# Recurrent preparation: another order of the bonus factor, the rows of r and k, the exponentials and the key norm's root

## What is computed

```
w = -softplus(-(w0 + tanh(xw @ w_lora1) @ w_lora2)) - 0.5;  log_decay = -exp(w)
a = sigmoid(a0 + (xa @ a_lora1) @ a_lora2)
kk = heads(k * k_k)
kk = kk / maximum(sqrt(sum(kk * kk, axis=-1)), 1e-12)      # the key norm
k = k * (1 + (a - 1) * k_a)
y = scan(r, log_decay, k, v, -kk, kk * a)                  # state of 64 x 64 per head
bonus = sum(r * k * r_k, axis=-1) * v
```

## Time and profile before

| | us |
|---|---|
| median of 3 runs (lowest to highest) | 4425.35 (4421.27 to 4426.27) |
| profiled execution | 4427.14 |
| its span, first to last instruction | 4425.4 |
| PE busy in the span | 4140.4 (94%) |
| VectorE busy | 3212.2 (73%) |
| ScalarE busy | 1564.6 (35%) |
| GpSimd busy | 698.8 (16%) |

### The profile page before, as it was taken

One profiled execution on the slowest core, in us unless ns is written; L12 is line 12 of the kernel. 1 busy time (PEld: TensorE's weight loads), 2 busy tenths in 40 slices (PEclk: granted clock), 3 DMA queues, 4 the chain that ended last, 5 costly groups with the idle time before them and its releaser, 6 DMA issues. The chain is left out here.

```text
span 4425.4 us, 62371 instructions
## 1 busy us (share of the span) xinstructions
PE 4140.4 (94%) x23580; PEld 3705.0 (84%) x23580; DVE 3212.2 (73%) x4912; ACT 1564.6 (35%) x2731; POOL 698.8 (16%) x580
## 2 busy tenths in 40 slices
PE   8999989978988999898978999999999999999995
PEld 6888875657766877787767999999999999999995
DVE  4444437757835445699095889988999999889997
ACT  2111213436623322222373333333333333333333
POOL 0000001113310100234500111111111111111110
PEclk9999999999999999899999999999999999999998
DMA  9999996886786487674368999999999999999996
GB/s 277 316 313 315 313 268 176 246 244 184 209 216 212 129 253 223 206 220 143 128 173 273 313 322 321 312 317 317 314 315 321 319 317 317 315 315 318 318 316 215
DMA packets 609083, 1176.94 MB, mean 266 GB/s; under 512 B 113944, under 2 KB 363648, under 8 KB 554160
## 3 DMA queue, kind: packets, MB, share of 16 engines
q1 hardware_dynamic: 534992, 800.28, 61.6%
q0 software_dynamic: 54256, 363.92, 21.7%
q10 hardware_dynamic: 19568, 9.18, 0.8%
HBM read 1006.90 MB, written 228.15 MB: 279 GB/s over the span
## 5 line engine op out<-in xcount | busy, mean ns | idle before, releaser
L102 PE MATMUL h_ps<-h_a,h_v 128*128 128x352 f32 x6144 | 1080.7, 324 | 22.5 <-DVE h_a L96 12.6
L102 PE MATMUL h_ps<-xs,h_ut 128*128 128x352 f32 x6144 | 1078.2, 324 | 17.3 <-DVE h_ut L96 17.3
L102 PEld LDWEIGHTS h_ps<-h_a,h_v 128*128 128x128 f32 x6144 | 1005.4, 189 | 31.5 <-DVE h_a L96 17.8
L102 PEld LDWEIGHTS h_ps<-xs,h_ut 128*128 128x128 f32 x6144 | 1010.7, 188 | 18.0 <-DVE h_ut L96 18.0
L102 PE MATMUL a_ps<-xt_hi,a_w 128*128 128x512 f32 x1792 | 553.1, 390 | 8.0 <-DVE a_w L96 8.0
L96 DVE TENSOR_TENSOR h_v<-h_v_raw,h_v 128x512 fp32r<-128x512 f32 x512 | 350.3, 684 | 73.7 <-ACT h_v L95 73.6
L102 PEld LDWEIGHTS a_ps<-xt_hi,a_w 128*128 128x128 f32 x1792 | 337.1, 188 | 78.3 <-issue 8.2
L95 ACT ACTIVATE h_v<-h_v_raw 128x512 fp32r<-128x512 f32 x512 | 318.2, 622 | 215.5 <-PE h_ps L102 212.4
L102 PE MATMUL a_ps<-xt_lo,a_w 128*128 128x512 f32 x896 | 349.2, 390 | 0.0
L2810 DVE SCALAR_TENSOR_TENSOR y_first<-h_rows,h_acts,y_first 128x2048 f32<-128x2048 f32 x128 | 300.2, 2345 | 0.0
L2804 DVE CUSTOM_DVE_ANT_0 h_rows<-h_rows,h_x_first 128x2048 f32<-128x2048 f32 x128 | 292.2, 2283 | 0.0
(11 more groups left out here) (385 smaller groups left out, 6452.7 us busy)
## 6 DMA issues: line engine op xcount, KB each, us to landing
h_v_raw<-in_peer_v SPq DMA_DIRECT2D x128, 1024.0 KB, 10.0
h_u_raw<-turned_d SPq DMA_DIRECT2D x138, 512.0 KB, 10.2
raw_d<-in_peer_u SPq DMA_DIRECT2D x472, 128.0 KB, 3.8
h_u_raw<-raw_d SPq DMA_DIRECT2D x118, 512.0 KB, 9.9
a_raw<-in_w_in SPq DMA_DIRECT2D x28, 2048.0 KB, 12.8
a_xin<-in_peer_u SPq DMA_DIRECT2D x224, 256.0 KB, 8.1
turned_d<-a_xin SPq DMA_DIRECT2D x56, 1024.0 KB, 7.0
yt_last<-sums_d SPq DMA_DIRECT2D x124, 176.0 KB, 5.3
```

Of the source, the lines that this page charges most:

```text
L102: mm = pe.matmul(out, lhs[a], rhs[b], start=(first and n == 0), stop=(last and n == 2))
```

## The change

The order inside a turn changes on two engines; no instruction is added or taken away. On ScalarE the three exponentials stand ahead of the root. On VectorE `rk_part` stands right behind `k_new`, ahead of the lower halves of "square"; `r_row`, `k_row` and `decay_end` stand behind those halves and ahead of the wait for the root; then come the norm, `kk`, `kk_a`, `a_row` and `b_row`, and only then the lower halves of "bonus". `kk_a` is now waited for. PE's list is the same.

```diff
--- before.py
+++ after.py
@@ -457,10 +457,10 @@
         p1dve = Steps(s["dve"], DV0, "diff shift")
         AC1 = AC0 + 4
         pe_ = Steps(s["pe"], p1pe.end(MB), "decay_in rate_in gate_in square_sum bonus_sum chunks0 bk_turned v_turned chunks1")
-        ac_ = Steps(s["act"], AC1, "decay_sig rate log_decay square gate norm e_in e_out e_prev bk_copied v_copied")
+        ac_ = Steps(s["act"], AC1, "decay_sig rate log_decay square gate e_in e_out e_prev norm bk_copied v_copied")
         dv_ = Steps(s["dve"], p1dve.end(MB),
-                    "diff shift kk_raw cum cum_prev k_part k_new norm_max norm_inv kk kk_a rk_part "
-                    "a_row r_row b_row k_row decay_end bonus masked0 masked1 masked2 masked3")
+                    "diff shift kk_raw cum cum_prev k_part k_new rk_part r_row k_row decay_end norm_max norm_inv "
+                    "kk kk_a a_row b_row bonus masked0 masked1 masked2 masked3")
 
         @block.gpsimd
         def _(pool):
@@ -667,12 +667,12 @@
                     act.wait_ge(s["st_g"], 16 * m)
                 c.mark("gate", act.copy(gs[:, :], ps[:, 2, :]))
                 pieces(m, "square")
-                act.wait_ge(s["pe"], pe_.at(m, "square_sum"))
-                c.mark("norm", act.activation(nrm[:, :], ps[:, 3, :], ACT.Sqrt))
                 act.wait_ge(s["dve"], dv_.at(m, "cum_prev"))
                 c.mark("e_in", act.activation(e_in[:, :], cum[:, :], ACT.Exp))
                 c.mark("e_out", act.activation(e_out[:, :], cum[:, :], ACT.Exp, scale=-1.0))
                 c.mark("e_prev", act.activation(e_prev[:, :], cumx[:, :], ACT.Exp))
+                act.wait_ge(s["pe"], pe_.at(m, "square_sum"))
+                c.mark("norm", act.activation(nrm[:, :], ps[:, 3, :], ACT.Sqrt))
                 pieces(m, "bonus", "turned")
                 act.wait_ge(s["pe"], pe_.at(m, "bk_turned"))
                 if m >= 1:
@@ -737,26 +737,26 @@
 
                 c.then("k_part", dve.tensor_scalar(k2[:, :], av[:, :], par(9, m), ka1[:, m:m + 1], ALU.mult, ALU.add))
                 c.then("k_new", dve.tensor_tensor(k2[:, :], k2[:, :], k[:, :], ALU.mult))
+                if m >= 1:
+                    dve.wait_ge(s["st_bon"], 16 * m)
+                c.then("rk_part", dve.scalar_tensor_tensor(tmp[:, :], r[:, :], par(10, m), k2[:, :],
+                                                           ALU.mult, ALU.mult))
                 pieces(m, "square")
+                dve.wait_ge(s["act"], ac_.at(m, "e_prev"))
+                if m >= 1:
+                    dve.wait_ge(s["st_ar"], 32 * m)
+                c.mark("r_row", dve.tensor_tensor(ar[:, :, 1, :], ch3(r[:, :]), ch3(e_in[:, :]), ALU.mult))
+                c.mark("k_row", dve.tensor_tensor(bk[:, :, 1, :], ch3(k2[:, :]), ch3(e_out[:, :]), ALU.mult))
+                c.mark("decay_end", dve.tensor_copy(dec[:, m, :], ch3(e_in[:, :])[:, :, L - 1]))
                 dve.wait_ge(s["act"], ac_.at(m, "norm"))
                 c.then("norm_max", dve.tensor_scalar(nrm[:, :], nrm[:, :], 1e-12, None, ALU.max))
                 c.then("norm_inv", dve.reciprocal(nrm[:, :], nrm[:, :]))
                 c.then("kk", dve.tensor_tensor(kk[:, :], kk[:, :], nrm[:, :], ALU.mult))
-                c.mark("kk_a", dve.tensor_tensor(dif[:, 0, :], kk[:, :], av[:, :], ALU.mult))
-                if m >= 1:
-                    dve.wait_ge(s["st_bon"], 16 * m)
-                c.then("rk_part", dve.scalar_tensor_tensor(tmp[:, :], r[:, :], par(10, m), k2[:, :],
-                                                           ALU.mult, ALU.mult))
-                pieces(m, "bonus")
-                dve.wait_ge(s["act"], ac_.at(m, "e_prev"))
-                if m >= 1:
-                    dve.wait_ge(s["st_ar"], 32 * m)
+                c.then("kk_a", dve.tensor_tensor(dif[:, 0, :], kk[:, :], av[:, :], ALU.mult))
                 c.mark("a_row", dve.scalar_tensor_tensor(ar[:, :, 0, :], ch3(kk[:, :]), -1.0, ch3(e_prev[:, :]),
                                                          ALU.mult, ALU.mult))
-                c.mark("r_row", dve.tensor_tensor(ar[:, :, 1, :], ch3(r[:, :]), ch3(e_in[:, :]), ALU.mult))
                 c.mark("b_row", dve.tensor_tensor(bk[:, :, 0, :], ch3(dif[:, 0, :]), ch3(e_out[:, :]), ALU.mult))
-                c.mark("k_row", dve.tensor_tensor(bk[:, :, 1, :], ch3(k2[:, :]), ch3(e_out[:, :]), ALU.mult))
-                c.mark("decay_end", dve.tensor_copy(dec[:, m, :], ch3(e_in[:, :])[:, :, L - 1]))
+                pieces(m, "bonus")
                 dve.wait_ge(s["pe"], pe_.at(m, "bonus_sum"))
                 c.mark("bonus", dve.tensor_tensor(bon[:, :], ps[:, 3, :], v[:, :], ALU.mult))
                 pieces(m, "turned")
```

## The result

The changed kernel takes 4450.35 us (median of 4 runs, 4444.42 to 4451.49) against 4423.34 us of the kernel before (4 runs of the same comparison): ratio 1.006 with a 95% interval from 1.0047 to 1.0073, so 21 to 32 us slower. The forecast was 4455 in a range of 4440 to 4468.

What follows compares the result with a forecast made beforehand. PE was taken to set the stage's pace, so edits on other engines count through its waits. 8 x (2.99 + 0.37) - 3.1 = 23.8 us plus 6.2 us of low clock gave 30.0 us slower: 4455 us, range 4440 to 4468.

Steps and rivals of the forecast that it cites:

- The root 2.99 us later: ScalarE: root behind the exponentials and a second load, 2.99 us later a turn, less 3.1 us over three turns.
- the rival with a load less: ScalarE: exponential runs from the sigmoid's table, saving 1.28 us a turn; about 20 us slower, 4445; chance 0.15 shared.
- the longer price for a load: ScalarE: the skill page's 2.7 us a table load would add about 1.4 us a turn, some 11 us in all.
- The bonus halves behind a_row and b_row, 0.37 us a turn: VectorE: first bonus half comes later, so PE's wait moves from bonus sum to first bonus piece; costs 0.37 us a turn.
- rk_part and the rows ahead of the norm cost nothing and bring nothing: VectorE: early `rk_part` and rows fit into waits, costed at nothing; PE reaches L592 after the rows end anyway.
- The clock, 6.2 us: PE: long waits in turns 3, 4 and 7 newly bring the low clock, 3 x 2.05 = 6.2 us; ends 0 and 10.3.
- The sum: Whole loop: 23.8 us without the clock plus 6.2 us for it, 30.0 us slower.
- the first term: Loop without the clock: 8 x (2.99 + 0.37) - 3.1 = 23.8 us.
- the rival "no change": Next turn gives the later bonus pieces back, for instance through earlier weights and root; about 4425, chance 0.05.
- The forecast of the waits,: PE before the bonus pieces (L102): about 4 us in turns 3, 4, 7 and about 6 in 1, 2, 5, 6.
- The rival that the wait really goes: PE: bonus halves ready by the early sum's end, 18.7 us of waiting and the clock go; 4398, chance 0.05.

Runs made afterwards that it cites:

- ScalarE's part alone: Kernel before with only ScalarE's order changed, the three exponentials ahead of the root; ratio 1.0062, 27 us slower, loop 26.3 us longer.
- VectorE's part alone: Kernel before with `rk_part` behind `k_new` and bonus halves behind `a_row` and `b_row`, ScalarE in its old order; 4425.27 us, ratio 1.0005.
- the two runs with the halves moved: Kernel before with `rk_part` early and both bonus halves, or only the first, behind the reciprocal; 4409.48 us (ratio 0.9965) and 4404.37 us (0.9955).
- the run with both halves behind the reciprocal: Kernel before with `rk_part` early and both bonus halves ahead of `kk`, ScalarE as before; 4409.48 us, ratio 0.9965.

## Why the prediction was right, step by step

- *The root 2.99 us later.* Right: from the table load's start to the root it is 825.25 - 820.97 = 4.28 us, as written. There is a load of 1.28 us ahead of each of the two functions, so the rival with a load less is out, and a function that waits for nothing else starts 0.01 or 0.02 us behind its load, so nothing of the longer price for a load that stood beside the sum appears. The run of ScalarE's part alone carries the term: 26.3 us of loop with the clock, against 27 expected.
- *The bonus halves behind a_row and b_row, 0.37 us a turn.* Right: the half starts 832.39 - 825.88 = 6.51 us behind `norm_max` (6.53 written), PE goes on 0.74 us later, and VectorE's part alone lengthens the loop by 3.0 us (8 x 0.37 = 3.0).
- *rk_part and the rows ahead of the norm cost nothing and bring nothing.* Right for the rows: they fill VectorE's wait (1.87 us ahead of them, 0.53 behind them). For `rk_part` it is right that it costs nothing visible (PE's waits at the square pieces are 3.1 us where they were 2.8). That it brings nothing holds only together with the halves' move: alone it shortens the loop by 8.0 us.
- *The clock, 6.2 us.* Right in the mechanism and a little low. In the changed kernel the eight times from the first bonus piece to L592 are 5.79, 8.12, 7.40, 8.43, 7.25, 8.13, 7.66 and 7.08 us, 13.5 us in all above turn 0's. All of turns 1 to 7 have the low clock, and turn 0, with a wait of 1.48 us, has not, as forecast. Before, L614 to L592 took 8.07, 9.25, 8.23 and 8.17 us in the four slow turns against 6.61 (the earlier trace rows and the two rows below), 7.3 us in all, and this includes the slow bonus sum itself. The difference is 6.2. The three new turns paid 5.4 of it where 3 x 2.05 was written; the mean of all four slow turns, 1.82, would have given 5.5. The low clock behind the square piece of turn 5 comes on top and stood nowhere in the sum: from L610 to L614 that turn takes 8.27 us without its wait and turn 1 takes 7.00, so about 1.3 us more. The clock's part is then about 7.5 us.

```profile
894.89 1.16 PE L592 MATMUL b_ps<-b_ar,b_bk 64*128 64x128 f32 x16
931.43 1.16 PE L592 MATMUL b_ps<-b_ar,b_bk 64*128 64x128 f32 x16
```

- *The sum.* 23.8 + 6.2 = 30.0 was written; the loop grew by 27.9 and the kernel by 27.0. Without the clock's 7.5 the first term measures about 20.4, 3.4 less than written; the two misses partly cancel, and that much of the agreement is luck. Where the 3.4 went can be read turn by turn, from L610 to L592 and without the clock. Turns 1, 2, 3, 4 and 7 grew by 3.4, 3.4, 3.1, 3.2 and 3.0 us, as the term has it (3.36, less 0.34 in turn 3 and 0.19 in turn 7 that the root had waited for PE). Turn 6 grew by only 2.1: ScalarE's last square half, which waits for its weights, came 1.47 us behind L610 where it had come 2.73, and the root gained by that. This is the mechanism of the rival "no change", in one turn of eight. Turn 5 grew by 2.8 and turn 0 by 0.3, where 0.75 was due. A wait of 0.8 us of L592 for a mask in turn 5 of the trace before is gone. The two traces of the kernel before differ among themselves in when that square half comes (2.0 and 2.6 us behind L610 in turn 2, 2.7 and 2.0 in turn 6), so part of this is the chance of one execution.
- *The forecast of the waits,* about 4 us in turns 3, 4 and 7 and about 6 in 1, 2, 5 and 6, was right (4.18, 4.71, 4.14; 6.11 three times) but for turn 5 (4.18; its square piece had waited 2.16 us before it, 0.9 more than in the trace of before).
- *The rival that the wait really goes* failed as forecast, because the half came late. It priced the wait and the clock at 27 us; the two runs with the halves moved get 18.7 and 18.2 us of it in the loop.

## What to carry to other kernels

Where an engine takes its list in order, making one operand early moves the wait to the next thing in the list that is late: look at what stands behind the waiting instruction and who makes that. Filler work for the busy engine needs its own operands early, ahead of any chain that the filler is meant to hide; here two halves of 0.7 us each stood behind a norm of 6 us. A reorder that puts an operation with a table of its own behind others pays the switch on the path. What counts is the time of the chain that ends last, not the number of loads, which did not change here.

## What the runs showed of the hardware

In this loop an idle PE was dearer than its idle time, by an amount that the wait alone does not fix. Over the traces of this loop, waits up to 1.76 us at the bonus pieces or the bonus sum left the granted clock at full speed. Between 1.9 and 3.4 us it went either way: a wait of 1.9 us in VectorE's part alone was followed by 7.34 us for the 24 matmuls up to L592, and one of 3.3 us in the same trace by the 5.78 us of full speed. From 3.45 us on it was 7.0 to 8.5 us each time. Three products with no use, put into the wait, took the low clock out of three turns, 1.3 to 2.6 us each. In the loop of the run with both halves behind the reciprocal the granted clock was 1.00 throughout, and of the 18.7 us won there some 7.3 are the clock's (what it cost before, by the times above).

A table load took 1.28 us of ScalarE each time, and the function behind it, where it waited for nothing else, started 0.01 or 0.02 us after it. The number of loads is three a turn in both orders; which function stands last made 26.3 us of the loop, by the run with ScalarE's order alone.
